# Adding expert rows in DRAM: two accumulating scatters a step instead of one row for each choice

## The reference, cut to what matters

```python
_, eidx = lax.top_k(sel, TOP_K)                      # 8 experts a token
gate = ...                                           # their weights
def expert_block(args):
    xb = h[tb]
    hid = jax.nn.silu(xb @ w_exp_gate[e]) * (xb @ w_exp_up[e])
    return (hid @ w_exp_down[e]) * gb[:, None]
routed = jnp.zeros_like(h).at[tok].add(outs.reshape(m_rows, d))
shared = (jax.nn.silu(h @ w_sh_gate) * (h @ w_sh_up)) @ w_sh_down
x = x + g2 * (routed + shared)
y = rms_norm(x, g_final)
```

## Time and profile before

| | us |
|---|---|
| median of 3 runs | 1402.15 |
| lowest and highest of the runs | 1396.7 and 1406.48 |
| the profiled execution's own time | 1399.79 |
| its span in the profile, first to last instruction | 1397.9 |
| PE busy in the span | 1248.8 (89%) |
| DVE, ACT, POOL busy | 447.2, 216.1, 148.3 |

### The profile page before, as it was taken

The page is one execution under the profiler, slowest core; times in us unless marked ns, Lnnn a source line. Parts: engine busy times, 40 slices in busy tenths (PEclk is TensorE's granted clock), DMA queues, the critical chain, the costliest instruction groups (busy, mean ns, idle before and its releaser), DMA issues. The chain is left out here.

```text
span 1397.9 us, 19431 instructions
## 1 busy us (share of the span) xinstructions
PE 1248.8 (89%) x5889; PEld 546.1 (39%) x5889; DVE 447.2 (32%) x1159; ACT 216.1 (15%) x422; POOL 148.3 (11%) x154
## 2 busy tenths in 40 slices
PE   3899999799946899989999998999999998999394
PEld 1344344466714344423333333333333333333131
DVE  3122231233413164652322322232232232232158
ACT  2100000322302111111111111111111111111100
POOL 2000000000000100100111111111111111111021
PEclk9999999755767899999999999999999999999778
DMA  9964100860097810069987999999899779777374
GB/s 328 366 241 183 62 0 1 281 178 1 8 283 229 304 73 30 4 265 355 383 338 285 373 413 412 370 345 415 317 391 408 280 300 419 294 285 260 108 307 203
DMA packets 65533, 352.87 MB, mean 252 GB/s; under 512 B 11538, under 2 KB 11538, under 8 KB 32230
## 3 DMA queue, kind: packets, MB, share of 16 engines
q1 hardware_dynamic: 48526, 311.15, 58.7%
q0 software_dynamic: 15680, 37.05, 7.0%
q10 hardware_dynamic: 1240, 3.78, 0.7%
HBM read 337.24 MB, written 34.13 MB: 266 GB/s over the span
## 5 line engine op out<-in xcount | busy, mean ns | idle before, releaser
L1182 PE MATMUL psum<-sb_stream,sb_convg 128*64 128x512 f32 x1664 | 376.5, 606 | 22.4 <-DMA sb_stream<-w_exp_up 20.8
L1182 PEld LDWEIGHTS psum<-sb_stream,sb_convg 128*64 128x64 f32 x1664 | 120.1, 140 | 235.3 <-issue 233.7
L1208 PE MATMUL psum<-sb_stream,sb_aT 128*64 128x512 f32 x832 | 190.0, 598 | 0.0
L1313 POOL DMA_INDIRECT expert_rows<-sb_attn,sb_row x52 | 52.4, 1007 | 542.5 <-DVE sb_token L1142 287.7
L1600 DVE TENSOR_TENSOR sb_aT<-psum,sb_aT 128x256 f32<-128x256 f32 x53 | 22.5, 425 | 227.3 <-ACT sb_aT L1386 227.3
L1208 PEld LDWEIGHTS psum<-sb_stream,sb_aT 128*64 128x64 f32 x832 | 55.1, 136 | 95.4 <-issue 89.3
L613 PE MATMUL psum<-sb_hT,sb_stream 128*128 128x512 f32 x192 | 86.3, 606 | 2.8 <-DMA sb_stream<-w_in 2.8
L1628 DVE TENSOR_SCALAR sb_attn<-psum,sb_now_gate 128x512 f32<-128x512 f32 x52 | 39.0, 751 | 148.9 <-PE psum L1208 148.9
L677 PE MATMUL psum<-sb_stream,sb_hT 128*128 128x512 f32 x192 | 86.2, 606 | 0.0
L1386 ACT ACTIVATE sb_aT<-psum 128x256 f32<-128x256 f32 x53 | 20.4, 384 | 387.3 <-PE psum L1182 386.0
L1156 PEld LDWEIGHTS psum<-sb_cst,sb_work 128*128 128x128 f32 x424 | 51.3, 194 | 43.0 <-issue 43.0
(11 more groups left out here) (285 smaller groups left out, 1155.4 us busy)
## 6 DMA issues: line engine op xcount, KB each, us to landing
sb_stream<-w_exp_gate SPq DMA_DIRECT2D x65, 1024.0 KB
sb_stream<-w_exp_up SPq DMA_DIRECT2D x65, 1024.0 KB
sb_stream<-w_exp_down SPq DMA_DIRECT2D x65, 1024.0 KB, 10.9
sb_stream<-w_ada SPq DMA_DIRECT2D x12, 2048.0 KB, 18.5
sb_stream<-expert_rows SPq DMA_DIRECT2D x8, 2048.0 KB, 13.8
sb_stream<-w_in SPq DMA_DIRECT2D x6, 2048.0 KB, 14.8
sb_stream<-cache_k SPq DMA_DIRECT2D x8, 1024.0 KB, 18.6
sb_stream<-cache_v SPq DMA_DIRECT2D x8, 1024.0 KB, 13.5
```

The costliest lines, as they stand in the source:

```text
L1182: last = pe.matmul(psum[lo:lo + LANE, 0, :].rearrange("p (a n) -> p a n", a=2), xT[:, k, lo:lo + LANE], gu[j][:, k, :, :], start=(k == 0), ...
L1208: last = pe.matmul(psum[lo:lo + LANE, 4 + n, :], hidT[:, k, lo:lo + LANE], dn[j][:, k, n * 512:(n + 1) * 512], start=(k == 0), stop=(k == 1))
L1313: pool.indirect_dma_start(expert_rows, bass.IndirectOffsetOnAxis(ap=row[:, u, :], axis=0), out[:, u, :], None, bounds_check=last_expert_ro ...
```

## The change

The array `expert_rows` goes. In its place stand two DRAM arrays of token sums, one a lane, 544 rows each. The first starts as the shared expert's rows (ACT stores each tile when it is made), the second as zeros (SP stores five tiles of zeros ahead of the first expert weights, POOL clears their source). In each step POOL issues two indirect DMAs that add onto these arrays, by the token's number: one of 64 partitions for lane 0, one of 128 partitions for lane 1, with the indices of its first 64 partitions out of bounds. Each waits until the scatter of the same lane of the step before has landed, so that no two additions to one row are under way together; POOL's counter `go` tells DVE's `place` when index buffers are free. The row column and the running sum leave the table. At the end of stage 3 SP waits for the last scatters and reads both arrays, two rows a token; stage 4 adds the two in PSUM, DVE takes the gate multiplication straight from PSUM, and the scaling by the inverse root moves to ACT.

```diff
+    for j in range(LANES):
+        c[:, C_AT + j] = np.where(p // LANE == j, OUTSIDE, 2 * OUTSIDE)
...
-    expert_rows = nc.dram_tensor("expert_rows", (NTOK * TOPK, D), F32, kind="Internal").ap()
+    sums = [nc.dram_tensor(f"sum{j}", (NTOK, D), F32, kind="Internal").ap() for j in range(LANES)]
...
+        both = stream[:, 0:NT * LANES * D].rearrange("p (t j n) -> p t j n", t=NT, j=LANES)
...
             @block.sync
...
+                sp.wait_ge(s["zeroed"], 4)
+                for t in range(NT):
+                    sp.dma_start(sums[1][t * P:t * P + rows(t), :], nothing[0:rows(t), :]).then_inc(sum_init[1], 16)
                 nb = trips(sp)
...
+                for j in range(LANES):
+                    sp.wait_ge(scat[j], 32 * nb)
+                for t in (NPT, *range(NPT)):
+                    for j in range(LANES):
+                        sp.dma_start(both[0:rows(t), t, j, :], sums[j][t * P:t * P + rows(t), :]).then_inc(sums_in[t], 16)
             @block.gpsimd
...
+                pool.wait_ge(s["h2_ok"], NT)
+                pool.memset(nothing, 0.0).then_inc(s["zeroed"], 1)
...
+                for j in range(LANES):
+                    pool.wait_ge(sum_init[j], 16 * NT)
                 nb = trips(pool)
+                def add_rows(j, u):
+                    n = (j + 1) * LANE
+                    pool.indirect_dma_start(sums[j], bass.IndirectOffsetOnAxis(ap=row[0:n, j, u, :], axis=0),
+                                            out[0:n, u, :], None, bounds_check=last_row, oob_is_err=False,
+                                            compute_op=ALU.add).then_inc(scat[j], 16)
...
-                                pool.indirect_dma_start(expert_rows, bass.IndirectOffsetOnAxis(ap=row[:, u, :], axis=0),
-                                                        out[:, u, :], None, bounds_check=last_expert_row,
-                                                        oob_is_err=False).then_inc(scat[u], 16)
+                                for j in range(LANES):
+                                    if c:
+                                        pool.wait_ge(scat[j], 16 * b)
+                                        pool.sem_inc(s["go"], 1)
...
+                                    add_rows(j, u)
             @block.scalar
...
-                act.wait_ge(s["zeroed"], 3)
+                act.wait_ge(s["zeroed"], 4)
...
+                    act.wait_ge(s["out_lo"], t + 1)
+                    act.wait_ge(s["out_hi"], t + 1)
+                    act.dma_start(sums[0][t * P:t * P + r, :], ysh[0:r, t, :]).then_inc(sum_init[0], 16)
             @block.vector
...
-                    total = running(run[0], run[1], 96, mask)
-                    step(v.tensor_tensor(table[:, :, :, 5], total[..., 32:], mask, ALU.subtract))
...
                 def place(c):
-                    v.tensor_scalar(row[:, c % 2, :], got[:, c % 3, 1:2], float(TOPK * OUTSIDE), None, ALU.add).then_inc(s["now_ok"], 1)
+                    for j in range(LANES):
+                        v.tensor_scalar(row[:, j, c % 2, :], got[:, c % 3, 0:1], cst[:, C_AT + j:C_AT + j + 1], None,
+                                        ALU.add).then_inc(s["now_ok"], 1)
...
-                                    v.wait_ge(scat[u], 48 * i + 16 * (c // 2))
-                                    place(c)
+                                v.wait_ge(s["go"], 4 * b + 3)
+                                place(c)
...
     def stage_4(x2, both, sums_in, gate2, gfin, ss, work):
...
+                    act.activation(work[0:r, j % 2, :], x2[0:r, t, :], ACT.Copy, scale=ss[0:r, 2, t:t + 1]).then_inc(scaled, 1)
...
+                        for a in range(LANES):
+                            last = pe.matmul(psum[0:r, 2 * (j % 2) + n, :], ident[0:r, 0:r], both[0:r, t, a, cols],
+                                             start=(a == 0), stop=(a == LANES - 1))
...
+                def finish(j):
+                    r = rows(order[j])
+                    y = work[0:r, j % 2, :]
+                    v.wait_ge(scaled, j + 1)
+                    v.tensor_tensor(y, y, gfin[0:r], ALU.mult).then_inc(y_ok, 1)
...
+                    v.wait_ge(added, j + 1)
+                    step(v.tensor_tensor(y, psum[0:r, b:b + 2, :].rearrange("p a n -> p (a n)"), gate2[0:r, t // NPT, :], ALU.mult))
                     v.sem_inc(sum_read, 1)
                     step(v.tensor_tensor(x2[0:r, t, :], x2[0:r, t, :], y, ALU.add))
                     step(v.tensor_tensor_reduce(y, x2[0:r, t, :], x2[0:r, t, :], 1.0, 0.0, ALU.mult, ALU.add, ss[0:r, 0, t:t + 1]))
                     step(v.tensor_scalar(ss[0:r, 1, t:t + 1], ss[0:r, 0, t:t + 1], 1.0 / D, EPS, ALU.mult, ALU.add))
                     v.sem_inc(ms, 1)
+                    if j:
+                        finish(j - 1)
+                finish(NT - 1)
```

More of the change, by code:

```diff
@@ L57 @@
 C_FOLD = C_POW + 1
-C_END = C_FOLD + NS
+C_AT = C_FOLD + NS
+C_END = C_AT + LANES
 A_PM, A_PN = 0, 512
@@ L1031, in stage_3 @@
         ysh = flat[:, 0:NT * D].rearrange("p (t n) -> p t n", t=NT)
+        nothing = flat[:, NT * D:(NT + 1) * D]
         h2T = tmp("h2T", [P, KC, NTOK])
@@ L1091, in stage_3 @@
         gath = [sem(f"s3_gath{i}") for i in range(2)]
-        scat = [sem(f"s3_scat{i}") for i in range(2)]
+        scat = [sem(f"s3_scat{j}") for j in range(LANES)]
+        sum_init = [sem(f"s3_sum_init{j}") for j in range(LANES)]
+        sums_in = [sem(f"s3_sums_in{t}") for t in range(NT)]
         ROUNDS = -(-TRIPS // 3)
@@ L1776, in _, with stage_4 @@
                 down_lanes(pe, 1, lambda n: pe.wait_ge(s[("out_lo", "out_hi")[n]], blocks - 1 + NT))
-        stage_4(x2, ysh, gate2, gfin, room[:, 3 * D:3 * D + 3 * NT].rearrange("p (a t) -> p a t", a=3), work)
+        stage_4(x2, both, sums_in, gate2, gfin, room[:, 3 * D:3 * D + 3 * NT].rearrange("p (a t) -> p a t", a=3), work)
         st.close()
-    def stage_4(x2, ysh, gate2, gfin, ss, work):
-        ring = stream[:, 0:3 * TOPK * D].rearrange("p (s k n) -> p s k n", s=3, k=TOPK)
-        H = TOPK // 2
+    def stage_4(x2, both, sums_in, gate2, gfin, ss, work):
         order = [NPT, *range(NPT)]
-        two_ok, sums, sum_read, y_ok, ms, rs = (sem(f"s4_{n}") for n in ("two_ok", "sums", "sum_read", "y_ok", "ms", "rs"))
-        first_in = [sem(f"s4_first{i}") for i in range(3)]
-        second_in = [sem(f"s4_second{i}") for i in range(3)]
+        added, sum_read, scaled, y_ok, ms, rs = (sem(f"s4_{n}") for n in ("added", "sum_read", "scaled", "y_ok", "ms", "rs"))
         y_out = [sem(f"s4_y_out{i}") for i in range(2)]
         v_step = sem("s4_v_step")
-        rows_of = expert_rows.rearrange("(n k) d -> n k d", k=TOPK)
         with nc.Block() as block:
@@ L1794, in _ @@
                 for j, t in enumerate(order):
-                    r = rows(t)
-                    if j >= 3:
-                        sp.wait_ge(y_ok, j - 2)
-                    for a, signal in ((0, first_in), (H, second_in)):
-                        sp.dma_start(ring[0:r, j % 3, a:a + H, :],
-                                     rows_of[t * P:t * P + r, a:a + H, :]).then_inc(signal[j % 3], 16)
+                    sp.wait_ge(y_ok, j + 1)
+                    dst = (io["y_prompt"][0, t * P:(t + 1) * P, :] if t < NPT else
+                           io["y_sample"].rearrange("b t n -> (b t) n"))
+                    sp.dma_start(dst, work[0:rows(t), j % 2, :]).then_inc(y_out[j % 2], 16)
+                sp.wait_ge(y_out[0], 3 * 16)
+                sp.wait_ge(y_out[1], 2 * 16)
                 sp.wait_ge(stored, 16 * n_stores[0])
@@ L1833, in _ @@
                     r = rows(t)
[L1834 removed]
+                    pe.wait_ge(sums_in[t], 32)
                     if j >= 2:
@@ L1838, in _ @@
                         cols = slice(n * 512, (n + 1) * 512)
-                        pe.matmul(psum[0:r, 2 * (j % 2) + n, :], ident[0:r, 0:r], ysh[0:r, t, cols], start=True, stop=False)
-                        for k in range(H):
-                            last = pe.matmul(psum[0:r, 2 * (j % 2) + n, :], ident[0:r, 0:r], ring[0:r, j % 3, k, cols],
-                                             start=False, stop=(k == H - 1))
-                    last.then_inc(sums, 1)
+                        for a in range(LANES):
+                            last = pe.matmul(psum[0:r, 2 * (j % 2) + n, :], ident[0:r, 0:r], both[0:r, t, a, cols],
+                                             start=(a == 0), stop=(a == LANES - 1))
+                    last.then_inc(added, 1)
             @block.vector
```

93 lines of the change are left out of this document (33 added, 60 removed).

## The result

The changed kernel takes 1413.9 us (median of 8 runs, 1409.9 to 1416.7) where the kernel before took 1400.9 on the same chip: a ratio of 1.0091, 95% interval 1.0069 to 1.0113. It is 0.9% slower, where 1393 us and so a small gain was forecast; the time lies in the stated range. Its profiled execution took 1410.1 us, its span is 1408.2, 10.3 more than before.

The account below looks back on a forecast made before the run. PE was taken to bound the loop nearly everywhere, the DMA engines as well in half of the steps; the end waits for reads, then DVE. 1399.8 - 34.4 - 1.5 + 28 = 1392, stated as 1393 us, range 1366 to 1436.

Parts of the forecast that it names:

- The last part: Stage 4 after the loop: reads covered inside stage 3, PE starting with the stage, fewer DVE additions; 34.4 us less, bounds 30 to 40.
- Ahead of the loop: Before the expert loop: DVE work and a PE wait go, a memset and a store come; net -1.5 us, bounds -3 and +2.
- Steps and hand-offs: In each loop step: `place` waiting for POOL fits in DVE's 3.78 us of idle time and costs nothing; landings have time enough.
- The DMA engines: In the loop's steps: adding needs a second read, unevenly spread; 21 steps x 1.35 = 28 us more, bounds 0 and +88.
- a second read of 4 KB for each row scattered: In each loop step: adding onto a row reads its old value, 0.9 us of DMA time a step if evenly spread.
- the middle, 1.35 us: DMA cost added to a loop step, taken between 0.9 (rows evenly spread) and 1.8 us (half of the engines loaded).
- half of the engines carry lane 1: Rival on the loop's scatters: half of the engines carry all of lane 1, 1.8 us in 21 steps, 38 us: 1402; chance 0.15.
- The hidden read: Rival: the second read goes on while other transfers are under way, 0 to 8 us for the loop: 1364 to 1372; chance 0.27.
- Costs three times: Rival: an added row costs three times a plain one, every loop step bound by the DMA engines: 1419 to 1452; chance 0.22.
- The landing: Rival: waiting for the same lane's scatter to land sets the loop's beat; 1443 at landings of 15.5 us; chance 0.06.
- A DMA share of over 0.95 in the loop: Sign that the forecast is right: the DMA engines' share over the loop rises above 0.95, from 0.89.
- The sign for the DMA step itself: A loop of 654 us, or one above 710, would make the forecast's added DMA time in the loop wrong.

Follow-up runs that it names:

- e3: Changed kernel with one adding scatter of 128 rows a step, into one array holding both lanes' sums, in place of two scatters: 1392.7 us, ratio 0.9933.
- e4: As e3 but with the scatter plain, so the additions of expert rows are left out: 1363.8 us, ratio 0.9730.
- e1: Changed kernel with both lanes' adding scatters spanning 128 partitions, the other lane's half of the indices out of bounds: 1395.8 us, ratio 0.9954.
- e8: e4 with one more indirect DMA a step that reads lane 0's rows only, half of all, by a list of 64 indices: 1387.4 us, ratio 0.9898.
- e9: As e8, the same extra rows read by a list of 128 indices whose second half is out of bounds: 1388.2 us, ratio 0.9919.
- e14: Changed kernel with only lane 1's scatter adding, lane 0's plain and over 128 partitions, its second half out of bounds: 1395.8 us, ratio 0.9939.
- e7: e4 with one more indirect DMA a step that reads as many rows from another array into an unused spare buffer: 1397.5 us, ratio 0.9961.
- e12: Changed kernel with only lane 0's scatter adding, over 128 partitions with its second half out of bounds, lane 1's plain: 1383.5 us, ratio 0.9855.
- e6: Kernel before the change, with the reads of the last part's first three tiles issued by SP at the end of stage 3: 1394.8 us, ratio 0.9937.

## Why the prediction was wrong, point by point

*The last part: right, -34.4 forecast, -38.8 measured.* PE started 33.6 us behind the last gate/up start (34.5 forecast), at the stage's start and not behind its reads, and the reads were covered as said. The third tile was the step that was off: three tiles at the lower clock were assumed, and the windows of the changed kernel have it at 0.50 for the first tile (the lower level, after PE's pause), 0.59 for the second, and 1.00 from the third on. DVE's beat from there is 5.36 us a tile (5.5 forecast).

```profile
1369.00:1376.10 7.10, 7.06 (x9) 1.35 (x9) 0.00 (x0) 0.00 (x0) 0.00 (x0) 0.50 1.01 408
1376.10:1381.50 5.40, 5.40 (x8) 2.34 (x9) 3.79 (x5) 0.60 (x1) 0.57 (x1) 0.59 0.06 25
1381.50:1386.00 4.50, 4.50 (x11) 1.92 (x11) 3.83 (x5) 0.55 (x1) 0.00 (x0) 1.00 0.00 0
```

*Ahead of the loop: -1.5 forecast, +0.1 measured.* It cannot be judged: kernels that differ only behind this place start their loops between 627.5 and 633.6 us.

*Steps and hand-offs: right.* Undisturbed steps keep 12.28 us, DVE's idle time went to 2.13 (1.4 to 2.7 forecast), POOL's third DMA and the landing waits (12.1 at most) do not show. PE's wait for weights is 57.6 us (some 50 forecast).

*The DMA engines: 28 us forecast, 49 measured.* This step failed, in two terms. The text priced "a second read of 4 KB for each row scattered" at 0.9 us a step if evenly spread, in 21 steps: 19 us. As DMA time that is right: 0.98 us by the queue, 18.4 us of waits (e3 against e4). What was left out is the clock. The analysis of the kernel before named it ("the rest is the lower clock in parts of these stretches"), but the sum priced a longer wait by its length alone; each is followed by slow products, 11.2 us in all. The second term is the spread: "I take the middle, 1.35 us" gave the uneven load 0.45 x 21 = 9 us. The full case of the rival, 0.9 x 21 = 19, is what it is: 16.8 us more of waits and 2.1 of PE's busy time in the changed kernel than in e3. 18.4 + 11.2 + 18.9 are 48.5 of the 48.7 between the changed kernel and e4. (The loop is PE's busy time and its waits, so such a sum closes; what the runs show is how it splits.) So "half of the engines carry lane 1", held at 0.15, is the rival that e1 and the counts of the scatters bear out, with e8, e9 and e14 left unexplained. With the clock's 12 its 1402 would have been 1414 on the profile's scale, where 1410.1 was measured and the last part had gained 4.4 more than forecast.

The Trainium skill had something on both. In "DMA: Bandwidth & Descriptors", the descriptor swizzle, partitions 64 to 127 of a transfer to 128 partitions are written by engines 8 to 15; the trace agrees in so far as a half-filled list keeps eight of its sixteen counts 1.11 us apart from the others, and it names no engine. In "Collectives: The Full Stack", part 3, the bandwidth ceiling, a reduce-scatter, which reads two sources for each chunk, is slower than an all-gather by 1.93; here the 52 scatters went from 47.6 us of engine time (an estimate, the prediction's share of the queue) to 47.6 + 50.8 = 98.4, a factor of 2.07.

*The other rivals.* The hidden read is refuted by e3 and e7. "Costs three times" is refuted by 2.07; that the loop lost 49 / 21 = 2.3 us a step, close to the 2.4 at which it was to be 1% slower, comes of the spread and the clock. The landing did not become the beat.

*The signs.* A DMA share of over 0.95 in the loop was given as a sign and did not come: it is 0.90. The share is a mean of all steps and of 16 engines: the slow step above has 0.41 of it, and of an uneven load it shows nothing (0.92 in e3, where the load is even). In PE's longest wait of the changed kernel it is 1.01, in one of e3's 1.00. A sign for an uneven load must not be a mean over the engines. The sign for the DMA step itself, a loop of 654 or above 710 us, was too wide: 703.5 lies inside it, 21 over the 654.5 + 28 of the sum.

```profile
1112.39:1120.18 7.79, 0.00 (x2) 0.03 (x1) 2.20 (x11) 0.16 (x1) 4.41 (x3) 0.62 1.01 356
```

```profile
1098.00:1103.73 5.73, 0.00 (x1) 0.04 (x1) 2.02 (x10) 0.10 (x1) 2.63 (x2) 0.76 1.00 409
```

## What to carry to other kernels

Price a DMA that adds as a read and a write of its rows, and look where its rows lie in the list of 128 partitions. Here a half-filled list of 128 loaded eight engines, which also carried a part of the list of 64 beside it; one full list with an offset in the index did not. A wait added to PE costs its length and the slow products that come after it; in this loop 12 us on 36.8 of waits. When the queue's engine time and the stall disagree between two versions, the mean over 16 engines may hide the spread.

## What was not expected of the hardware

- Adding in the two lanes is not equally dear: e14 (lane 1 added) took 1395.8 us, its mirror image e12 (lane 0 added) 1383.5, at the same engine time. Lane 1 differs from lane 0 in its half of the list, and also in that its scatter is the second of the step. No run changed the order, so the cause stays open.
- An adding scatter holds POOL for longer: 1.59 us with 128 indices (e3) against 1.01 plain (e4).
- In e6 SP issued the early reads 9.1 us behind the start of the last scatter, whose last count stands in the trace at 1308.97, 3.7 us behind that start. The chain of waits has SP's queue still at the conditions of the loop (L1263, L1265), whose last rounds are empty, until just before. To issue these reads from another engine was not tried. The timeline, and then the chain (start, us, what):

```profile
1305.23 1.00 POOL L1323 DMA_INDIRECT expert_rows<-sb_attn,sb_row  x1 [3.71 <-DVE sb_attn L1638]
1314.32 2.70 SPq L1278 DMA_DIRECT2D sb_stream<-expert_rows  x6
```

```profile
1312.06 1.95 issue
1314.01 0.03 SPq L1263
...
1314.32 4.71 DMA sb_stream<-expert_rows
```
